# The row roots of a first RMS norm: eight broadcast transposes, or one transpose and a trip through DRAM

## The reference

```python
def rms_norm(x, g):
    y = x * lax.rsqrt(jnp.mean(x * x, axis=-1, keepdims=True) + EPS)
    return y * g

h = rms_norm(x, mix_norm_g)
u_a, v_a, q, k, v = jnp.split(h @ w_in, splits, axis=-1)    # 512, 512, 512, 128, 128 columns
y_a = spatial_gating(u_a, v_a, ...)        # gelu, layer norm of v_a, 128x128 position mixing
y_b = window_sink_attention(q, k, v, ...)
x = x + concat(rms_norm(y_a), rms_norm(y_b)) @ w_out
h = rms_norm(x, ffn_norm_g)
x = x + (silu(h @ w_gate) * (h @ w_up)) @ w_down
return rms_norm(x, final_norm_g)
```

## Time and profile before

| | before |
|---|---|
| time, median of 3 runs | 917.71 us |
| the profiled execution's own time | 917.77 us |
| its span | 916.0 us |
| PE busy | 908.3 us (99% of the span), 4224 matmuls |
| DVE busy | 586.9 us (64%) |
| ACT busy | 429.4 us (47%) |
| POOL busy | 394.7 us (43%) |
| DMA | 158.56 MB, 173 GB/s over the span |

### The profile page before, as it was taken

The page is one execution under the profiler, slowest core; times in us unless marked ns, Lnnn a source line. Parts: engine busy times, 40 slices in busy tenths (PEclk is TensorE's granted clock), DMA queues, the critical chain, the costliest instruction groups (busy, mean ns, idle before and its releaser), DMA issues.

```text
span 916.0 us, 11952 instructions
## 1 busy us (share of the span) xinstructions
PE 908.3 (99%) x4224; PEld 749.4 (82%) x4224; DVE 586.9 (64%) x783; ACT 429.4 (47%) x835; POOL 394.7 (43%) x387
## 2 busy tenths in 40 slices
PE   9999999999999999999999999999999999999997
PEld 7888888787878888888888888888888888888885
DVE  6559979986679776465464655636537566544754
ACT  6647448856556533333333333333335554444451
POOL 1459633331243478557485575855754000000021
PEclk9999999999999999999999999999999999999999
DMA  9797553221343272643726437264367996566543
GB/s 333 239 261 233 120 164 104 74 77 63 102 129 100 85 229 73 227 142 123 230 76 224 141 124 230 81 219 147 118 221 262 375 357 195 197 187 201 187 138 138
DMA packets 151211, 158.56 MB, mean 173 GB/s; under 512 B 27696, under 2 KB 108656, under 8 KB 151152
## 3 DMA queue, kind: packets, MB, share of 16 engines
q1 hardware_dynamic: 150480, 157.40, 53.3%
q10 hardware_dynamic: 672, 0.40, 0.1%
HBM read 117.26 MB, written 40.50 MB: 172 GB/s over the span
## 4 chain that ended last, share of the span: by engine, by line
PE 98%; issue 1%; ACT 0%; POOL 0%; DVE 0%; POOLq 0%; ACTq 0%
PE ps L853 31%; PE ps L855 31%; PE ps L854 31%; PE ps L1017 1%; PE ps L1040 1%; PE ps L965 1%; PE ps L1029 1%; PE ps L1111 1%; PE ps L877 0%; PE ps L886 0%; PE ps L889 0%; PE ps L892 0%; PE ps L986 0%; PE ps L976 0%; PE ps L1047 0%
## 5 line engine op out<-in xcount | busy, mean ns | idle before, releaser
L2096 DVE TENSOR_TENSOR P_lo<-P_raw,P_hi 128x512 fp32r<-128x512 f32 x132 | 119.4, 919 | 83.5 <-ACT P_hi L1538 77.8
L854 PE MATMUL ps<-T_lo,P_hi 128*128 128x512 f32 x352 | 137.1, 389 | 0.0
L855 PE MATMUL ps<-T_hi,P_lo 128*128 128x512 f32 x352 | 137.1, 389 | 0.0
L853 PE MATMUL ps<-T_hi,P_hi 128*128 128x512 f32 x352 | 137.1, 389 | 0.0
L795 POOL TENSOR_TENSOR wd<-wd 128x256 f32<-128x256 f32 x88 | 82.6, 939 | 91.5 <-DMA wd<-in_w_down 86.3
L855 PE MATMUL ps<-rb_hi,ra_lo 128*128 128x512 f32 x308 | 120.0, 390 | 0.0
L853 PE MATMUL ps<-rb_hi,ra_hi 128*128 128x512 f32 x308 | 120.0, 389 | 0.0
L854 PE MATMUL ps<-rb_lo,ra_hi 128*128 128x512 f32 x308 | 119.9, 389 | 0.0
L1652 ACT ACTIVATE ra_hi<-ra 128x512 fp32r<-128x512 f32 x77 | 48.6, 631 | 98.3 <-DMA rb<-w_down_T 61.9
L643 POOL TENSOR_SCALAR late<-late 128x1 f32<-128x1 f32 x12 | 6.0, 504 | 191.9 <-ACT junk L1720 178.3
L2205 DVE TENSOR_TENSOR ra_lo<-ra,ra_hi 128x512 fp32r<-128x512 f32 x77 | 55.3, 718 | 35.4 <-ACT ra_hi L1652 35.0
(11 more groups left out here) (280 smaller groups left out, 2017.4 us busy)
## 6 DMA issues: line engine op xcount, KB each, us to landing
wd<-in_w_down SPq DMA_DIRECT2D x44, 256.0 KB, 3.4
w_down_T<-wd SPq DMA_DIRECT2D x22, 512.0 KB, 4.6
ra<-act_S SPq DMA_DIRECT2D x44, 256.0 KB, 2.7
rb<-w_down_T SPq DMA_DIRECT2D x44, 256.0 KB, 3.0
act_S<-Q SPq DMA_DIRECT2D x33, 256.0 KB, 3.7
ra<-act_A SPq DMA_DIRECT2D x33, 256.0 KB, 4.8
rb<-in_w_down SPq DMA_DIRECT2D x33, 256.0 KB, 5.7
P_raw<-in_w_gate SPq DMA_DIRECT2D x22, 256.0 KB, 3.6
```

The lines of the kernel that those rows point to most:

```text
L853: mm(dst, lhs[0], rhs[0], start=start, stop=False, skip_group_check=onto)
L854: mm(dst, lhs[0], rhs[1], start=False, stop=False, skip_group_check=onto)
L855: return mm(dst, lhs[1], rhs[0], start=False, stop=stop, skip_group_check=onto)
L2096: tt(w_l[p, m][:], src[:], w_h[p, m][:].bitcast(F32), ALU.subtract).then_inc(w_split, 1)
```

## The change

The eight transposes and both copies go. In their place: GpSimd computes the second four roots behind the 22nd of its 29 small copies, before `rel_built`; PE makes one transpose of all eight columns behind block k = 5, which gives eight rows of 128 roots in PSUM; ACT copies these 8 by 128 numbers to SBUF, stores them to DRAM (4 KB), waits for the landing, and issues one load that reads the 4 KB once for each of the 128 partitions (512 KB in all) into both roots tiles. This stands behind the store of `by_offset` and ahead of the `gated_rows` of the second half. Every `evict` waits for this load.

```diff
-    roots = [at("roots0", 184, [P, C]), at("roots1", 186, [P, C])]
+    roots_all, root_rows = at("roots", 184, [P, 2, C]), at("root_rows", 206, [T, P])
+    roots = [roots_all[:, h] for h in range(2)]
+    root_dram = nc.dram_tensor("row_roots", [T, P], F32, kind="Internal")
@@ GpSimd, in the loop over the copies into by_offset
+                if n == 3 * len(runs) // 4:
+                    x_roots(1)
             last.then_inc(rel_built, 1)
-            x_roots(1)
@@ TensorE
-            def roots_T(h):
-                pe.wait_ge(x_rstd, h + 1)
-                pe.wait_ge(v_ready, HT * h + 3 + h)
-                for t in range(HT):
-                    r = HT * h + t
-                    last = nc.tensor.transpose(ps[:, ROOT_BANK[h], t * P:(t + 1) * P], rstd_x[:, r:r + 1].to_broadcast([P, P]), ident[:])
-                last.then_inc(rstd_T, 1)
@@ behind gate_block(1, k)
-                    roots_T(0)
+                if k == 5:
+                    pe.wait_ge(x_rstd, 2)
+                    nc.tensor.transpose(ps[0:T, ROOT_BANK, 0:P], rstd_x, ident[:]).then_inc(rstd_T, 1)
@@ in_product("P1", i)
+                    elif i == 2:
+                        pe.wait_ge(root_rows_ready, 1)
                     else:
-                        pe.wait_ge(roots_ready, i - 1)
+                        pe.wait_ge(v_ready, T)
@@ behind unit(0)
-                if j == 0:
-                    roots_T(1)
@@ ACT, behind the store of by_offset
-            roots_copy(0)
+            act_e.wait_ge(rstd_T, 1)
+            actv(root_rows[:], ps[0:T, ROOT_BANK, 0:P], ACT.Copy).then_inc(root_rows_ready, 1)
+            act_e.wait_ge(root_rows_ready, 1)
+            act_e.dma_start(root_dram.ap(), root_rows[:]).then_inc(roots_out, 16)
+            act_e.wait_ge(roots_out, 16)
+            act_e.dma_start(roots_all[:].rearrange("p h n -> p (h n)"), root_dram.ap().rearrange("t p -> (t p)").partition_broadcast(P)).then_inc(roots_in, 16)
             for r in range(HT, T):
                 gated_rows(r)
-            roots_copy(1)
@@ DVE, evict(j)
-                dve.wait_ge(roots_ready, half + 1)
+                dve.wait_ge(roots_in, 16)
```

More of the change, by code:

```diff
@@ L296, in hybrid_trunk_layer @@
     WARM = 15
-    ROOT_BANK, MIX_BANK = (2, 7), (3, 4)
+    ROOT_BANK, MIX_BANK = 2, (3, 4)
     STORES = [[slice(0, D)]] * (T - 1) + [[slice(0, C), slice(C, D)]]
@@ L315, in hybrid_trunk_layer @@
         x_in = [sem(f"x_in{s}") for s in range(4)]
-        x_sq, x_mse, x_rstd, rstd_T, roots_ready, hT0_hi_ready, hT_hi_ready, hT_ready = (
-            sem(n) for n in ("x_sq", "x_mse", "x_rstd", "rstd_T", "roots_ready", "hT0_hi_ready", "hT_hi_ready", "hT_ready"))
+        x_sq, x_mse, x_rstd, rstd_T, root_rows_ready, roots_out, roots_in, hT0_hi_ready, hT_hi_ready, hT_ready = (
+            sem(n) for n in ("x_sq", "x_mse", "x_rstd", "rstd_T", "root_rows_ready", "roots_out", "roots_in", "hT0_hi_ready", "hT_hi_ready", "hT_ready"))
         block_in = [sem(f"block_in{k}") for k in range(K)]
@@ L1274, in _ @@
             act_e.dma_start(bias_dram.ap()[:, :, 0:CH + WIN - 1], by_offset[:, :, 0:CH + WIN - 1]).then_inc(bias_out, 16)
-            def roots_copy(h):
-                act_e.wait_ge(rstd_T, h + 1)
-                actv(roots[h][:], ps[:, ROOT_BANK[h], :], ACT.Copy).then_inc(roots_ready, 1)
-            roots_copy(0)
+            act_e.wait_ge(rstd_T, 1)
[4 more added lines that the diff above has]
+            act_e.dma_start(roots_all[:].rearrange("p h n -> p (h n)"), root_dram.ap().rearrange("t p -> (t p)").partition_broadcast(P)).then_inc(roots_in, 16)
             for r in range(HT, T):
                 gated_rows(r)
-            roots_copy(1)
             def in_weight_hi(p, i):
```

## The result

| | before | after |
|---|---|---|
| median | 917.70 us (9 runs, 917.31 to 918.13) | 919.27 us (9 runs, 918.28 to 921.70) |
| the profiled execution's own time | 917.77 us | 918.67 us |
| its span | 916.0 us | 916.9 us |

The ratio is 1.0021, 95% interval 1.0012 to 1.0029: the change makes the kernel 1.6 us slower. The predicted 919.2 us is met by the median, and the profiled execution lies 0.9 us above that of before. That is not the whole of 1.6 us, and the runs after spread four times as wide as the runs before. So two things have to be explained: the 0.9 us that the profile shows, and the rest.

What follows compares the result with a forecast made beforehand. PE's stream bounds the kernel, but at 75 us PE waits for the fourth eviction, set by by_offset's store and the bytes ahead of D2. 917.77 + 0.4 (store) + 1.0 (broadcast) gave 919.2 us; range 917.4 to 921.0.

Steps and rivals of the forecast that it cites:

- What bounds the kernel: At P1's second product PE waits for the fourth eviction, behind D2's loads, losing 0.11 us; no wait that shows behind 75 us.
- PE's saving is worth nothing: PE reaches P1's second product 0.71 us sooner, but all of it goes into the wait for the fourth eviction.
- Term a: The by_offset store, issued 1.29 us later, delays bias_out and SP's loads behind it by 0.4 us (bounds 0 and 1.29).
- Term b: The 512 KB broadcast load's bytes, on the DMA engines ahead of D2, delay it by 1.0 us (0.73 to 1.33).
- The sum: The fourth eviction ends 1.4 us later, at 76.5; PE waits 2.2 us; the profiled execution takes 919.2 us.
- What is hidden: ACT's wait for the 4 KB store and gated_rows 0.8 us later cost nothing: 2.8 us in hand at unit 3.
- 2 (the load is dear): Ahead of D2, the broadcast runs at 225 GB/s and takes 2.3 us; eviction 3.2 us late, 921.0 us; chance 0.21.
- 1 (the transfers are hidden): Ahead of D2, the store lands when it did before and the load fills idle DMA time: 917.5 us; chance 0.20.

Runs made afterwards that it cites:

- before_early_root: The kernel before, with only the second four roots computed ahead of the last seven small copies: 917.96 us, ratio 1.0002.
- other_source: The changed kernel, with the broadcast load reading the final norm's gains, an input, in place of the stored 4 KB: 920.20 us, ratio 1.0024.
- root_late: The changed kernel, with the second four roots back behind the last copy and the one transpose behind block k = 6: 919.40 us, ratio 1.0022.
- before_plus_trip: The kernel before, plus a 4 KB store, ACT's wait for its landing and a 512 KB broadcast of it into an unread buffer: 918.57 us.

## Why the prediction was right, and what it missed

- *What bounds the kernel*: right. The fourth eviction is the place where the change holds PE up, and D2's landing sets it. With the eviction earlier the loss was gone, and PE's shift of 0.92 us at 76.19 is the span's difference. That no engine behind 75 us makes PE wait holds for the kernel before; with the fourth eviction out of the way, two waits at 93 to 97 us took its place in the changed one.
- *PE's saving is worth nothing*: right. 0.57 us of it reach P1's second product (0.71 was the estimate; 0.2 us were lost at the start of the program, where the first matmuls waited a little longer). The added transpose cost 0.11 us; 0.17 was the estimate.
- *Term a, the store of by_offset, 0.4 us*: too large. The store went out 1.3 us later, as predicted, but took 3.8 us in place of 5.3, and SP went on 0.2 us sooner, just below the lower bound of no shift; before_early_root found nothing either. The prediction's own working for the lower bound, that a later store meets fewer loads, fits what was measured, and it was given too little weight.
- *Term b, the broadcast's bytes, 1.0 us*: right in size, 0.7 us with the load alone and 1.0 in the runs at full clock after. It counts that the load stands ahead of D2, and not what it reads (other_source) or where exactly it stands (root_late). The prediction priced bytes on busy DMA engines; the trace shows the time in SP's issues, 2.32 us for two loads in place of 1.06, and that bytes and not packets or loads are what counts is not shown.
- *The sum, 1.4 us on the profiled execution*: its own came out at 0.9, since term a was nothing; PE lost 1.60 us from start to start where 2.2 were forecast, and the eviction ended at 76.04 in place of 76.5, between the 75.5 and 77.2 that the prediction named as the limits of being right. The median of 919.27 us fell on the forecast of 919.2 because a cost that was not in the sum, the lower clock in four of nine runs, took the place of term a. The mechanism was right; that the number was met is luck.
- *What is hidden*: right. `gated_rows` at 49.00 (49.2 predicted), `evict(0)` at 56.02 straight behind `v_centre`, the roots' load landed 4.5 us from its issue at 48.53, so at 53.0, no wait at units 2 and 3. The 3.0 us for the 4 KB store were met as well (45.50 to 48.53), but not for the reason of the sum: the store came in some 0.2 us behind the large one ahead of it. In root_late it was issued at 48.17, when the large one had 0.8 us to go, and ACT went on at 49.43, after 1.3 us.
- *The rivals*: 2 (the load is dear) has its size in the highest runs, but not its mechanism. 1 (the transfers are hidden) was right about the store, that is about term a. What was not among them is the clock, though the forecast itself had PE idle for 2.2 us. A forecast in which a saving turns into idle time should have asked what that does to the clock.

## What to carry to other kernels

A saving on the busiest engine is worth what the next wait on it leaves; where a wait that doesn't depend on that engine stands just behind, as a gap of 0.1 us in the timeline tells, the saving is lost whole. A tile that is broadcast by DMA is written in all partitions: 4 KB became 512 KB and cost 0.6 to 1.0 us, because it stood ahead of loads for which others wait. And an idle stretch of TensorE can have a second price: here it went with a lower clock in some runs, which shows in the spread of the runs and in their granted clock, and in none of the profiles.

## What was not expected of the hardware

Runs of one kernel on one chip differed by up to 4.9 us (918.08 to 922.95 in before_plus_trip), with the mean granted clock at 0.996 or 0.997 in the high ones, in kernels whose profile has PE waiting, beyond the program's start, just once: for 0.3 to 2.3 us, some 75 us in. Without that wait the runs stayed within 2.3 us in every kernel, and within 1.8 us in the kernel before.

The four low parts of P1's weights took 2.49 us after, from 56.62, where they took 5.79 from 57.43. POOL's timeline before has its subtractions of D1 beside them:

```profile
57.50 6.88 POOL L679 TENSOR_TENSOR D_raw<-D_raw,xb 128x512 f32<-128x512 f32 x4 [2.62 <-DMA xb<-in_xT]
```

After, these came later, for the later loads, and the low parts had DVE's time nearly to themselves:

```profile
58.23 5.78 POOL L682 TENSOR_TENSOR D_raw<-D_raw,xb 128x512 f32<-128x512 f32 x4 [2.71 <-DMA xb<-in_xT]
```

The same four instructions beside a busy POOL took over twice the time. The profiles of the experiments agree: where POOL begins within 0.6 us of them, they take 5.4 to 5.8 us, and where it begins 1.4 us or more behind them, 2.5 to 3.6.
